# A hybrid attention, RG-LRU and Hyena layer with experts: the order of loads and vector work ahead of the projection

## The reference, cut to what matters

```
sh1, sc1, g1, sh2, sc2, g2 = split(silu(cond) @ w_mod + b_mod, 6)   # one vector per condition
u = layer_norm(x) * (1.0 + sc1) + sh1
z = u @ w_in                                                        # 2816 columns: q, k, v, xr, gate, hy
h = sin(freq[0] * (feats @ w1 + b1))                                # Hyena's filter network
h = sin(freq[1] * (h @ w2 + b2))
filt = (h @ w3) * exp(-t * |decay|);  filt_f = rfft(circular(filt)) # the filter's spectrum
```

## Time and profile before

| what | value |
|---|---|
| device time, median of 3 | 634.93 us (634.59 to 637.37) |
| device time of the profiled execution | 633.17 us |
| its span | 631.3 us |
| mean granted TensorE clock | 0.997 |
| PE, busy share of the span | 95% |
| DVE | 70% |
| ACT | 48% |
| POOL | 30% |
| chain that ended last: PE, DVE, DMA, ACT | 82%, 7%, 5%, 4% |

### The profile page before, as it was taken

One profiled execution on the slowest core, in us unless ns is written; L12 is line 12 of the kernel. 1 busy time (PEld: TensorE's weight loads), 2 busy tenths in 40 slices (PEclk: granted clock), 3 DMA queues, 4 the chain that ended last, 5 costly groups with the idle time before them and its releaser, 6 DMA issues.

```text
span 631.3 us, 9327 instructions
## 1 busy us (share of the span) xinstructions
PE 600.8 (95%) x3353; PEld 455.3 (72%) x3353; DVE 440.5 (70%) x757; ACT 305.6 (48%) x506; POOL 188.4 (30%) x152
## 2 busy tenths in 40 slices
PE   6899999999999988998999999989999999999994
PEld 2237999999999965557888888747767677676352
DVE  4967766834994654467553499988998877983187
ACT  2748122335344543005795342846565655752354
POOL 1002333345551307041496070421212221321121
PEclk9999999999999999999999999999999999999998
DMA  9985852222221269764980706769999999999788
GB/s 305 387 305 222 305 186 97 101 101 100 101 68 66 92 238 325 303 264 99 290 271 36 294 8 234 280 168 370 393 376 403 390 388 406 374 364 372 291 299 144
DMA packets 40040, 154.89 MB, mean 245 GB/s; under 512 B 7049, under 2 KB 17033, under 8 KB 27451
## 3 DMA queue, kind: packets, MB, share of 16 engines
q1 hardware_dynamic: 27912, 115.41, 50.6%
q10 hardware_dynamic: 5522, 23.48, 9.4%
q0 software_dynamic: 6560, 15.42, 8.3%
HBM read 141.59 MB, written 23.63 MB: 262 GB/s over the span
## 4 chain that ended last, share of the span: by engine, by line
PE 82%; DVE 7%; DMA 5%; ACT 4%; issue 2%; POOL 0%; DVEq 0%; ACTq 0%; POOLq 0%
PE bank L1898 13%; PE bank L1574 12%; PE bank L1575 12%; PE bank L1770 9%; PE bank L1952 8%; PE bank L1410 3%; PE bank L1747 2%; PE bank L1674 2%; PE bank L1880 2%; DMA arena<-in_w_mod 2%; PE bank L1477 2%; PE bank L1625 2%; PE bank L2011 2%; PE bank L1730 2%; DMA u_scr<-arena 1%
## 5 line engine op out<-in xcount | busy, mean ns | idle before, releaser
L772 POOL TENSOR_TENSOR w_low<-arena,w_high 128x1024 fp32r<-128x1024 f32 x22 | 53.6, 2437 | 145.9 <-ACT w_high L971 145.9
L2544 DVE TENSOR_TENSOR gate_up_low<-arena,gate_up_high 128x1024 fp32r<-128x1024 f32 x64 | 75.3, 1221 | 12.3 <-ACT gate_up_high L1256 10.2
L1256 ACT ACTIVATE gate_up_high<-arena 128x1024 fp32r<-128x1024 f32 x64 | 63.9, 1054 | 15.5 <-DMA arena<-in_moe_w_gu 15.5
L971 ACT ACTIVATE w_high<-arena 128x1024 fp32r<-128x1024 f32 x22 | 23.2, 1058 | 87.8 <-PE bank L1575 87.0
L1574 PE MATMUL bank<-u_high,w_high 128*128 128x320 f32 x176 | 56.3, 320 | 1.7 <-DVE u_low L2157 1.7
L1952 PE MATMUL bank<-arena 128*128 128x512 f32 x128 | 57.7, 593 | 0.0
L1575 PE MATMUL bank<-u_high,w_low 128*128 128x320 f32 x176 | 54.4, 309 | 0.0
L1574 PE MATMUL bank<-u_high,w_low 128*128 128x320 f32 x176 | 54.4, 309 | 0.0
L1574 PE MATMUL bank<-u_low,w_high 128*128 128x320 f32 x176 | 54.4, 309 | 0.0
L1575 PE MATMUL bank<-u_low,w_high 128*128 128x320 f32 x176 | 54.4, 309 | 0.0
L1575 PE MATMUL bank<-u_high,w_high 128*128 128x320 f32 x176 | 54.4, 309 | 0.0
(11 more groups left out here) (442 smaller groups left out, 1396.4 us busy)
## 6 DMA issues: line engine op xcount, KB each, us to landing
arena<-in_moe_w_gu SPq DMA_DIRECT2D x38, 1024.0 KB, 10.1
arena<-in_w_mod SPq DMA_DIRECT2D x24, 1024.0 KB, 6.6
arena<-in_moe_w_down ACTq DMA_DIRECT2D x13, 1024.0 KB
arena<-in_w_in SPq DMA_DIRECT2D x11, 1024.0 KB, 4.8
arena<-in_moe_w_down SPq DMA_DIRECT2D x6, 1024.0 KB
y_scr<-arena SPq DMA_DIRECT2D x11, 512.0 KB, 9.1
arena<-in_x SPq DMA_DIRECT2D x10, 512.0 KB, 9.6
arena<-y_scr SPq DMA_DIRECT2D x10, 512.0 KB, 6.0
```

What stands on the lines that cost most here:

```text
L772: G.tensor_tensor(WL[s_][:, :, w], ring[s_][:, :, w], WH[m % 2].bitcast(F), ALU.subtract).then_inc(wl_rdy, 1)
L971: S.activation(WH[m % 2], ring[(m // 2) % 2][:, :, (m % 2) * P:(m % 2 + 1) * P], ACT.Copy).then_inc(wh_rdy, 1)
L1256: S.activation(WGH[j][c], raw_gu[s][:, c, :, :], ACT.Copy).then_inc(wgh_rdy, 1)
L2544: tt_(WGL[s][c], raw_gu[s][:, c, :, :], WGH[j][c].bitcast(F), ALU.subtract).then_inc(wgl_rdy, 1)
```

## The change

Four edits to the front; the rest of the kernel and its arithmetic are as before.

1. DVE takes the moments of one x tile (0) ahead of the second folding instead of two; tile 1 follows it with the others.
2. SP issues x tile 0, modulation block 0, x tiles 1 and 2, block 1, x tiles 3 and 4, and then blocks 2 to 7. Five buffers hold the blocks (the two others of the ring, `flat[2]` and `flat[0]`, are added), so blocks 0 to 4 wait for nothing, block 5 waits for block 0, and so on. Piece 0 of w_in waits until TensorE has used five blocks, piece 1 until it has used all eight (before, six; piece 0 had no wait of its own and stood behind block 7, which waited for five).
3. The filter's inputs are loaded as 33 rows of features and w1 and a separate load of w2; both count on `ld_filt`.
4. At the end of the u loop the order on DVE is `u_low(6)`, `spectrum_far(3)`, `u_low(7)`, `spectrum_near(3)`.

`front_dense` gets a parameter for its bank, and all its calls leave it at its value of before. The order of TensorE's program is the same.

```diff
-        filt = fl.take(NTOK + HIDDEN + P)
+        filt = fl.take(NTOK + HIDDEN)
+        w2 = fl.take(P)
...
+        mod1_in = mod_in + win_in
...
-        mod1_buf = [arena[:, MTAT:MTAT + 2048], arena[:, MTAT + 2048:MTAT + 4096], flat[1]]
+        mod1_buf = [arena[:, MTAT:MTAT + 2048], arena[:, MTAT + 2048:MTAT + 4096], flat[1], flat[2], flat[0]]
...
-            for i in range(TT):
-                eng.dma_start(X[:, i, :], t["x"][i * P:(i + 1) * P, :]).then_inc(ld_x[i], 16)
...
             def mod1_block(k):
-                if k >= 3:
-                    eng.wait_ge(mod1_mm, k - 2)
-                eng.dma_start(mod1_buf[k % 3], t["w_mod"][k * P:(k + 1) * P, 0:2048]).then_inc(mod_in[k % 3], 16)
+                if k >= 5:
+                    eng.wait_ge(mod1_mm, k - 4)
+                eng.dma_start(mod1_buf[k % 5], t["w_mod"][k * P:(k + 1) * P, 0:2048]).then_inc(mod1_in[k % 5], 16)
 
             def w_in_piece(p):
-                if p == 1:
-                    eng.wait_ge(mod1_mm, 6)
+                if p < 2:
+                    eng.wait_ge(mod1_mm, 8 if p else 5)
...
-            for k in range(KT):
+            def x_rows(i):
+                eng.dma_start(X[:, i, :], t["x"][i * P:(i + 1) * P, :]).then_inc(ld_x[i], 16)
+
+            for i in range(TT):
+                x_rows(i)
+                if i in (0, 2):
+                    mod1_block(i // 2)
+            for k in range(2, KT):
                 mod1_block(k)
...
-            eng.dma_start(filt, t["filt"]).then_inc(ld_filt, 16)
+            eng.dma_start(filt[0:FEATS, :], t["filt"]).then_inc(ld_filt, 16)
+            eng.dma_start(w2, t["hy_w2"]).then_inc(ld_filt, 16)
...
-                    eng.wait_ge(ld_filt, 16)
+                    eng.wait_ge(ld_filt, 32)
...
-            def front_dense(n):
+            def front_dense(n, bank=5):
...
             x_moments(0)
-            x_moments(1)
             filter_fold(1)
-            for i in range(2, TT):
+            for i in range(1, TT):
                 last = x_moments(i)
...
-                if k == 7:
-                    spectrum_far(3)
             u_low(KT - 2)
+            spectrum_far(3)
+            u_low(KT - 1)
             spectrum_near(3)
-            u_low(KT - 1)
```

More of the change, by code:

```diff
@@ L237, in build @@
         HF, FA, FB = (fl.take(SPAN) for _ in range(3))
-        filt = fl.take(NTOK + HIDDEN + P)
-        feats, w1, w2 = filt[:, 0:NTOK], filt[:, NTOK:NTOK + HIDDEN], filt[:, NTOK + HIDDEN:NTOK + HIDDEN + P]
+        filt = fl.take(NTOK + HIDDEN)
+        feats, w1 = filt[:, 0:NTOK], filt[:, NTOK:NTOK + HIDDEN]
+        w2 = fl.take(P)
         decay = fl.take(D)
@@ L500, in build @@
         flat = [r.rearrange("p a b -> p (a b)") for r in ring]
-        mod1_buf = [arena[:, MTAT:MTAT + 2048], arena[:, MTAT + 2048:MTAT + 4096], flat[1]]
+        mod1_buf = [arena[:, MTAT:MTAT + 2048], arena[:, MTAT + 2048:MTAT + 4096], flat[1], flat[2], flat[0]]
         mod2_buf = [flat[1], flat[2], flat[0]]
         def wait_w_in(eng, p):
-            eng.wait_ge(win_in[p % 2], 16 * (p // 2 + 1))
+            eng.wait_ge(win_in[p % 2], 16 * (p // 2 + 2))
         def ut_ctx_bank(k):
@@ L1413, in mod1 @@
             def mod1(k):
-                eng.wait_ge(mod_in[k % 3], 16 * (k // 3 + 1))
-                mod_block(B[4], k, mod1_buf[k % 3]).then_inc(mod1_mm, 1)
+                eng.wait_ge(mod1_in[k % 5], 16 * (k // 5 + 1))
+                mod_block(B[4], k, mod1_buf[k % 5]).then_inc(mod1_mm, 1)
             def filter_layer(layer):
@@ L1486, in ctx_spectrum @@
                 mm(B[3][:, :], TAPSc[1], OD[:, 0, :], start=True, stop=True).then_inc(spec_mm, 1)
-            def front_dense(n):
+            def front_dense(n, bank=5):
                 for b in range(n):
-                    mm(B[5][:, :], ident, consts[:, 2 * KT:2 * KT + 512], start=True, stop=True)
+                    mm(B[bank][:, :], ident, consts[:, 2 * KT:2 * KT + 512], start=True, stop=True)
             front_dense(1)
@@ L1593, in mod2 @@
             def mod2(b):
-                eng.wait_ge(mod_in[b % 3], 16 * ((3, 3, 2)[b % 3] + b // 3 + 1))
+                eng.wait_ge(mod_in[b % 3], 16 * (3 + b // 3))
                 mod_block(B[b // KT], b % KT, mod2_buf[b % 3]).then_inc(mod2_mm, 1)
@@ L2909 @@
     pair2[0:HIDDEN, 0:HIDDEN] = pair2[HIDDEN:P, HIDDEN:P] = a["hy_w2"][0]
-    filt = np.zeros((P, NTOK + HIDDEN + P), f32)
-    filt[0:FEATS, 0:NTOK] = features()
-    filt[0:FEATS, NTOK:NTOK + HIDDEN] = a["hy_w1"][0]
-    filt[:, NTOK + HIDDEN:] = pair2
+    filt = np.concatenate([features(), a["hy_w1"][0]], 1).astype(f32)
     rgw = np.zeros((P, 8, P), f32)
@@ L2938 @@
         "brt": np.concatenate([a["router_bg"][0], a["router_be"][0]]),
-        "filt": filt, "hy_w3": a["hy_w3"][0],
+        "filt": filt, "hy_w2": pair2, "hy_w3": a["hy_w3"][0],
         "decay": a["hy_decay"][0].reshape(-1), "dft_taps": spec_tables, "dft": fold_tables,
```

## The result

| | before | after |
|---|---|---|
| device time, median | 634.76 us (8 runs, 633.47 to 637.37) | 639.43 us (8 runs, 637.22 to 641.57) |
| ratio of the two | | 1.006, 95% interval 1.0044 to 1.0077 |
| profiled execution, its span | 633.17 us, 631.3 us | 639.69 us, 637.7 us |
| mean granted TensorE clock | 0.997 | 0.985 |

The changed kernel is slower, by 4.7 us in the medians. 635.5 was forecast, with 638.0 as the upper end of the range. The last row of the table points at the clock: the mean granted clock of all eight runs of the changed kernel lies between 0.982 and 0.988.

A forecast was written before the change was run, and what follows sets the result against it. PE, with 82% of the chain, was taken as the bound, so its entry into the dense projection counts. Terms 1.40 + 0.6 - 1.46 = +0.54 us on 634.93 gave 635.5 us, range 632.5 to 638.0.

The forecast's parts named there:

- TensorE's clock falls: Rival, chance 0.08: longer PE waits between block 0 and the last filter rows slow the clock, costing 3.9 us: 639.4.
- a wait of 1.68 us left the following eight instructions at 1.06 us: Trace observation held against a clock fall: PE's dense instructions after that wait ran as fast as an earlier block.
- the sum: The forecast's terms for the front added up: 1.40 + 0.6 - 1.46 = +0.54 us, with nothing for the clock.
- Edit 1, +1.40 us: Ahead of the last filter rows: tile 1's moments, before covered by DVE's wait for PE, come onto the path.
- Edit 2, +0.6 us: x loads behind two modulation blocks: tile 4 lands at 22.7, delaying DVE's last moments; term 0 to 1.2 us.
- its moments fit before: x tile 3, 512 KB or about 1.2 us ahead of tile 4 in SP's queue, was claimed not to delay DVE.
- my bound without saved bytes: Upper end for the x loads: tile 4 lands at 23.3 if the smaller filter load saves nothing, term 1.2 us.
- Edit 3, nothing: Filter inputs at the start of the front: one more load issue on ACT, at most half a us, costs nothing.
- the constants as unmoved: Constants' landing at the start of the front: no gain from fewer filter bytes beside them, range 0 to -0.6 us.
- Edit 4, -1.46 us: End of the u loop: `u_low(6)` fills DVE's idle time, so PE starts the last k at 63.33 instead of 64.79.
- w_in and the stores: nothing: Later w_in pieces and the stores of zeros behind them delay nothing in the front, with 7 us of cover.

The follow-up runs named there:

- edit 1 alone: Kernel before with only tile 1's moments moved behind the second folding: 639.26 us, ratio 1.0052.
- edit 3 alone: Kernel before with only the filter's inputs split into two loads: 635.13 us against 635.32, ratio 0.9985.
- dense matmuls in the waits: Changed kernel with three dense matmuls added in PE's two waits, their results overwritten: 634.60 us against 635.13, ratio 1.0004.
- one filter load: Changed kernel with the filter's inputs again loaded as one tile of 128 rows: 639.53 us, ratio 1.0067.
- edit 2 alone: Kernel before with only the new order of loads and five block buffers: 641.53 us, ratio 1.0087.
- edit 4 alone: Kernel before with only the low half put ahead of the odd spectrum: 633.62 us against 635.13; in a second group 633.11 against 635.22.

## Why the prediction was wrong

- **The outcome was a rival to which I gave 0.08.** "TensorE's clock falls" had its place (between block 0 and the last filter rows), its price (3.9 us; 4.15 measured) and its time (639.4; 639.43 measured). The step that failed is the argument against it, by which the sum put the clock at nothing: "a wait of 1.68 us left the following eight instructions at 1.06 us". That was one wait by itself at 248 us; PE's wait before it ended at 233 us. Here it is two waits with 2.3 us of work between them (1.61 and 1.23 us), and edit 1 alone showed that 1.17 and 1.37 us are enough. I also took the kernel before as safe, since the mean in its page is 0.997. The trace of edit 3 alone, with nearly the same waits, has a short fall, so it stood near the edge. In its 101 further runs eight have a mean clock below 0.9895 (median 638.2 us, 635.22 for all), which does not tell where they fell.
The Trainium skill ("TensorE: Matmul & The Clock Gate", HAM oscillation) tells of a kernel whose waits for loads, between bursts of matmuls, put the clock back to half each time. The waits here are for DVE's results, and otherwise the traces agree: the granted clock went to 0.50 behind them, and stayed at 1.00 when dense matmuls were put into them.
- **That 639.4 met 639.43 is in part luck.** The price was worked out from the slow start of the trace (2.2 us) and half of the time ahead of it, and no run shows that these have to do with the length of a fall. The sum under it holds 0.6 us for the loads, which cost nothing in the changed kernel. It lacks the 1.38 us of the late filter load and the slower dense group, and the 1.69 us of the fall at 420 us. The eight runs lie between 637.22 and 641.57 us.
- **Edit 1, +1.40 us: right in size and place** (24.92 and 29.81, with 1.39 of other delays), but its main cost is the clock: alone, 3.9 us in all.
- **Edit 2, +0.6 us: mis-sized.** I placed loads by bytes and had tile 4 decide, landed at 22.7 with moments ended at 24.1. By the same numbers tile 3, 1.2 us ahead of it, lands at 21.5 and is wanted at 20.6, so "its moments fit before" was a misreading: tile 3 decides, the moments end at 24.3, and the term is 0.8. In the changed kernel it did not bind at all, since folding 2 was late. Where that was on time, tile 3 did decide, at 21.3 to 22.8, and the moments ended at 24.6 (dense matmuls in the waits) and 25.7 (one filter load), where my bound without saved bytes gave 24.7. Less 22.12 and 1.40, the term measured 1.1 and 2.2 us there. That tile 1 lands late, at 13.0 to 14.8, had no part in my sum, and rightly, as edit 1 moves its use.
- **Edit 3, nothing: right in the sum, not in its parts.** Alone it has no effect in the medians, though the clock fell for short in its trace. I took the constants as unmoved (range 0 to -0.6). They landed at 4.48 in the changed kernel, and at 4.06 to 4.58 in the four other traces with edit 3, against 4.70 to 4.82 in the nine without it: 0.1 to 0.8 us earlier. The new second load gives this back where it is late: in the profiled execution it landed at 7.50 and cost 0.75 us, in another trace PE waited for it 0.33 us, in three not at all. I had bounded the constants, and not this load. The +0.63 us of the dense group is no effect of the change: it took 5.03 us (edit 1 alone) to 6.68 us (edit 2 alone), as PE came to its fast pace sooner or later.
The Trainium skill ("DMA: Bandwidth & Descriptors", SWDGE vs HWDGE vs iDMA) has each DMA engine go round-robin between its queues. I had read from it that the constants keep their share; that would need ACT's queue to be never empty beside them, which no run here shows. The landings decide.
- **Edit 4, -1.46 us: right**, 1.50 by the traces, 1.5 and 2.1 in the medians.
- **w_in and the stores: nothing, right.** ACT's copy of w_in had no wait in the changed kernel, POOL's halves were ready, and no wait for w_in is in PE's list.

## What to carry to other kernels

Where an edit lets TensorE wait longer, price the clock first: the longest wait does not decide by itself, since here one of 1.68 us left the clock alone and two of 1.17 and 1.37 us close together did not. Look at the granted clock of further runs of the kernel, not of one trace, and at where in the trace it fell. If the waits cannot be shortened, dense matmuls into a bank that is overwritten anyway can hold the clock; here three of them won back 4.8 us, with nine runs of ten at a mean of 0.993 or more. And before work is moved out of a wait, look which engine's wait covers it: moments in DVE's wait for PE were free, and 1.4 us behind it.

## What was not expected of the hardware

- Two waits of 1.17 and 1.37 us with some 2.2 us of matmuls between them brought the granted clock to 0.79 and 0.52 in the two stretches from 25 to 35 us in the trace of edit 1 alone, and all its ten runs have a mean of 0.984 to 0.989; in the trace of edit 3 alone one of 1.37 us, behind waits of 0.33 and 0.39, did it for a shorter stretch (0.89 and 0.77 in the two stretches from 25 to 35 us). With 0.2 and 1.4 us, in both traces of edit 4 alone, it stayed at 1.00.
- The length of the slow stretch did not follow the wait in these traces: 4.15 us were lost behind waits of 1.61 and 1.23, and 1.64 behind 2.64 and 1.38. How much one kernel's falls differ from run to run is not shown.
- Behind the same three waits, of 0.76, 0.57 and 0.89 us, the clock fell in one trace (0.66 from 420 to 425 us) and stayed at 1.00 in another.
- A load of 64 KB beside others landed 6.1 us after its issue (1.40 to 7.46) in one execution, 5.3 us after it in another, and before it was wanted in three.
